# Nine groups of mixer projections a layer as seven products each, with the weight sums on VectorE one group ahead

## The reference, cut to what matters

```python
(sq, sk, sv, dq, dk, dv, iq, ik, iw, hq, hf, hi, hg,
 g_sb, g_dsa, g_hg) = jnp.split(h @ w_in_l, _split_points(), axis=-1)
y_sb = stick_breaking_attention(heads(sq, N_SB), heads(sk, N_SB), heads(sv, N_SB)) @ w_sb_l
y_dsa = dsa_attention(q, k, dv, q_i, k_i, iw) @ w_dsa_l       # keeps the top 64 keys by an index score
o = hgrn2(heads(hq, N_HG), heads(hf, N_HG), heads(hi, N_HG), lb)   # q = silu(hq), a gated recurrence
mixed = sigmoid(g_sb) * y_sb + sigmoid(g_dsa) * y_dsa + sigmoid(g_hg) * y_hg
return mixed @ w_out_l
```

## Time and profile of the kernel before

| | |
|---|---|
| median of 3 runs | 1598.48 us (1598.16 to 1599.77) |
| the profiled execution | 1599.52 us, of it 1597.7 us span |
| PE busy / DVE busy / ACT busy | 1465.1 / 740.9 / 314.8 us |
| mixer steps of layer 0, from the last product of hf (92.31) to the first branch product (249.40) | 157.1 us |
| the same in layer 1 (565.36 to 719.46) | 154.1 us |
| expert weights, from about 1200 us on | DMA at 425 to 427 GB/s |

### The profile page before, as it was taken

One profiled execution on the slowest core, in us unless ns is written; L12 is line 12 of the kernel. 1 busy time (PEld: TensorE's weight loads), 2 busy tenths in 40 slices (PEclk: granted clock), 3 DMA queues, 4 the chain that ended last, 5 costly groups with the idle time before them and its releaser, 6 DMA issues.

```text
span 1597.7 us, 19690 instructions
## 1 busy us (share of the span) xinstructions
PE 1465.1 (92%) x8156; PEld 1006.0 (63%) x8156; DVE 740.9 (46%) x1465; ACT 314.8 (20%) x655; POOL 22.7 (1%) x41
## 2 busy tenths in 40 slices
PE   8999999999999999999999999999999576576578
PEld 5587889999544788898999445755554133133132
DVE  3646576766666646567666656544331000001001
ACT  2234431122001125430222001334410000000000
POOL 0000000000000000000000002200000000000000
PEclk9999999999999999999999999999999788788789
DMA  9547224454443633334444446755799999999997
GB/s 321 187 159 237 95 101 153 161 182 179 158 167 110 218 130 135 106 106 158 158 161 181 186 158 196 232 185 184 288 381 425 427 427 425 428 427 426 427 419 313
DMA packets 114921, 380.17 MB, mean 238 GB/s; under 512 B 10836, under 2 KB 23252, under 8 KB 104144
## 3 DMA queue, kind: packets, MB, share of 16 engines
q1 hardware_dynamic: 111952, 369.53, 60.7%
q0 software_dynamic: 2880, 9.36, 1.9%
HBM read 377.25 MB, written 5.73 MB: 240 GB/s over the span
## 4 chain that ended last, share of the span: by engine, by line
PE 32%; DMA 17%; SPq 1%; DVE 0%; ACT 0%; issue 0%; DVEq 0%
DMA ring<-in_w 17%; PE bank L1495 6%; PE bank L1541 6%; PE bank L1151 4%; PE bank L1692 4%; PE bank L1261 2%; PE bank L1590 2%; PE bank L1718 1%; SPq L928 1%; PE bank L1751 1%; PE bank L1187 1%; PE bank L1213 1%; PE bank L1200 1%; PE bank L1714 1%; PE bank L1648 0%; PE bank L1681 0%
## 5 line engine op out<-in xcount | busy, mean ns | idle before, releaser
L1144 PE MATMUL bank<-hT,ring 128*128 128x256 f32 x832 | 185.4, 381 | 0.0
L1144 PEld LDWEIGHTS bank<-hT,ring 128*128 128x128 f32 x832 | 156.0, 190 | 21.9 <-issue 1.0
L1692 PE MATMUL bank<-ring,region 128*32 128x512 f32 x208 | 115.7, 720 | 50.2 <-DMA region<-in_w 50.2
L1692 PE MATMUL bank<-region 128*32 128x512 f32 x512 | 115.8, 720 | 42.9 <-DMA ring<-in_w 42.9
L1541 PE MATMUL bank<-region 128*128 128x512 f32 x320 | 140.6, 592 | 0.0
L1541 PEld LDWEIGHTS bank<-region 128*128 128x128 f32 x320 | 60.5, 190 | 74.6 <-issue 74.6
L1495 PE MATMUL bank<-region 128*128 128x128 f32 x768 | 100.5, 275 | 0.0
L1495 PEld LDWEIGHTS bank<-region 128*128 128x128 f32 x768 | 93.0, 192 | 0.0
L1692 PEld LDWEIGHTS bank<-region 128*32 128x32 f32 x512 | 28.8, 129 | 87.4 <-issue 87.4
L1692 PEld LDWEIGHTS bank<-ring,region 128*32 128x32 f32 x208 | 25.7, 129 | 85.0 <-issue 85.0
L1751 PE MATMUL bank<-region 128*32 128x512 f32 x192 | 61.9, 748 | 15.7 <-DMA hT<-in_w 13.9
(11 more groups left out here) (486 smaller groups left out, 2413.7 us busy)
## 6 DMA issues: line engine op xcount, KB each, us to landing
region<-in_w SPq DMA_DIRECT2D x43, 2048.0 KB, 38.6
ring<-in_w SPq DMA_DIRECT2D x30, 2048.0 KB, 37.5
ring<-in_w_in SPq DMA_DIRECT2D x26, 2048.0 KB, 8.4
ring<-in_w_up SPq DMA_DIRECT2D x16, 2048.0 KB, 8.3
ring<-in_w_down SPq DMA_DIRECT2D x32, 1024.0 KB, 6.4
own_slot<-in_w SPq DMA_DIRECT2D x7, 2048.0 KB, 43.5
ring<-in_w_out SPq DMA_DIRECT2D x6, 2048.0 KB, 7.8
region<-in_w SPq DMA_DIRECT2D x22, 512.0 KB, 9.0
```

The source lines that it names most:

```text
L1144: t = mm(b[:, 0:T], w[:, k, :], act[:, k, :], start=(k == 0), stop=(k == KD - 1))
L1692: t = mm(b[32 * e:32 * e + 32, :], xg[:, k, 32 * e:32 * e + 32], four[e][c][:, 512 * (k % 2):512 * (k % 2) + 512], start=(k == 0), stop=(k ...
```

## The change

`hq`, `sk` with `sq`, and gate chunks 2 and 3 become nine "early" groups of seven products, numbered 0 to 8; the four groups of gate chunks 4 and 5 become groups 9 to 12. Gate tiles 0 to 7 stay plain. The sums of group n + 1 (`es`, four operations of 512 elements a partition) stand in the list beside the products of group n (`em`), ahead of the corners (`ec`) of group n. The whole-chunk sums `gw` go; `gt` stays, and a third set of row sums, `ge`, is made after `ln`. Groups 0 to 4 use the row sums that hf uses, 5 to 8 use `ge`, 9 to 12 use `gt`.

```diff
-LATE_GATES = 8
+PLAIN_GATES, LATE_GATES = 8, 8
+GROUPS = (("hq", 0), ("hq", 1), ("skq", 0), ("skq", 1), ("skq", 2),
+          (2, 0), (2, 1), (3, 0), (3, 1), (4, 0), (4, 1), (5, 0), (5, 1))
+EARLY, IN_HEADS = 9, 5
+GROUP_SUM = {"m5": 1, "m6": 3, "m7": 3, "m3": 4}
...
+    def em(n, *beside):
+        return [("em", n, m) for m in GATE_ORDER] + list(beside) + [("ec", n), ("ef", n)]
...
-    s += gm("hf", 1, *GATE_ORDER) + [("gc", "hf", 1), ("gf", "hf", 1), ("hq", 0)]
-    s += [("rt", c) for c in range(9)] + [("hj",)] + [("hq", m) for m in range(1, 4)]
+    s += gm("hf", 1, *GATE_ORDER) + [("gc", "hf", 1), ("gf", "hf", 1)]
+    s += [("es", 0)] + [("rt", c) for c in range(9)] + [("hj",)] + em(0, ("es", 1)) + em(1, ("es", 2))
     s.append(("hp",))
     half = N_IDX // 2
-    s += [("ix", 0, j) for j in range(half)] + [("sk", 0)] + [("ix", 0, j) for j in range(half, N_IDX)] + [("tk", 0)]
-    s += [("sk", m) for m in (1, 2)] + [("sq", m) for m in range(3)] + [("t5",)]
+    s += [("ix", 0, j) for j in range(half)] + em(2, ("es", 3))
+    s += [("ix", 0, j) for j in range(half, N_IDX)] + [("es", 4), ("tk", 0)]
+    s += em(3) + em(4) + [("t5",)]
     s += [("ix", 1, j) for j in range(N_IDX)] + [("tk", 1)]
-    s += [("z", c) for c in range(3)] + g(2) + [("ln",)] + g(2)
-    s += [("u", c) for c in range(3)] + g(2) + [("hs",), ("lv", 0), ("lv", 1), ("o", 0), ("o", 1)] + g() + [("o", 2)]
+    s += [("z", c) for c in range(3)] + g(2) + [("ln",), ("ge",)] + g(2)
+    s += [("u", c) for c in range(3)] + g(2) + [("hs",), ("lv", 0), ("lv", 1), ("es", 5), ("o", 0), ("o", 1)] + g() + [("o", 2)]
...
     for j in range(LEVELS):
         n = 3 if j < 4 else 2
-        s.append(("lm", j))
+        if j % 2 == 0:
+            s.append(("lm", j))
         s += att[at:at + n - 1]
         s += [("hx",)] if j == 0 else [("hl", j, 0)] if j < LEVELS - 1 else [("hl", j, 0), ("hl", j, 1)]
         if j + 2 < LEVELS:
             s.append(("lv", j + 2))
         s += att[at + n - 1:at + n]
         at += n
-        s += g(2 if j < 2 else 1)
-
-    s += [("gt",), ("gw", 4), ("ho",)]
+        if j % 2 == 0:
+            s += em(5 + j // 2, *([("lm", j + 1)] if j < LAST else []), ("es", 6 + j // 2))
+        elif j == 1:
+            s += g()
+
+    s += [("es", 10), ("gt",), ("ho",)]
     s += att[18:20] + gm(4, 0, *GATE_ORDER[:4]) + [att[20], ("on",), att[21]] + gm(4, 0, *GATE_ORDER[4:])
-    s += [("gw", 5), ("gc", 4, 0)] + att[22:] + gm(4, 1, *GATE_ORDER) + [("gc", 4, 1), ("gs",), ("gf", 4, 0), ("gf", 4, 1)]
+    s += [("gc", 4, 0), ("es", 11)] + att[22:] + gm(4, 1, *GATE_ORDER) + [("gc", 4, 1), ("es", 12), ("gs",), ("gf", 4, 0), ("gf", 4, 1)]
...
+            def early_product(l, n, m):
...
+                elif m == "m5" and n == IN_HEADS:
+                    pe.wait_ge(row_sums_ready, 3 * l + 2)
+                if m in GROUP_SUM:
+                    pe.wait_ge(group_sums_made, 4 * (len(GROUPS) * l + n) + GROUP_SUM[m])
...
                     elif kind == "z":
...
-                        wait_freed([(l, n, c) for n in ("sq", "sk")])
+                        pe.wait_ge(early_done, EARLY * l + c + 3)
...
+                    elif kind == "ec":
+                        A_(early_corners[:, 6, :], read((l, "ey", s[1]))[:, 0:P], ACT.Copy).then_inc(early_m1, 1)
+                    elif kind == "ef":
...
+                        act.wait_ge(*bk.freed((l, "ey", n)))
+                        if c == "hq":
...
+                            t = A_(hsg_both, early_corners[:, 0:4, :].rearrange("p c t -> p (c t)"), ACT.Sigmoid)
+                        elif c == "skq":
+                            A_(skT[:, t2, :], early_corners[:, 0:2, :].rearrange("p i t -> p (i t)"), ACT.Copy)
+                            t = A_(sqT[:, t2, :], early_corners[:, 2:4, :].rearrange("p i t -> p (i t)"), ACT.Copy, scale=HD ** -0.5)
...
+            def group_weight_sums(l, n):
...
+                elif n >= 2:
+                    dve.wait_ge(*group_done(l, n - 2))
+                (a11, a12), (a21, a22) = group_weights(l, n)
+                s1, s2, s3, s4 = group_sums(l, n)
+                at = 4 * (len(GROUPS) * l + n)
+                V.tensor_tensor(s1, a21, a22, ALU.add).then_inc(group_sums_made, 1)
+                V.tensor_tensor(s3, a11, a21, ALU.subtract).then_inc(group_sums_made, 1)
+                dve.wait_ge(group_sums_made, at + 1)
+                V.tensor_tensor(s2, s1, a11, ALU.subtract).then_inc(group_sums_made, 1)
+                dve.wait_ge(group_sums_made, at + 3)
+                V.tensor_tensor(s4, a12, s2, ALU.subtract).then_inc(group_sums_made, 1)
+
+            def early_corner_sums(l, n):
+
+                if EARLY * l + n >= 1:
+                    dve.wait_ge(early_done, EARLY * l + n)
```

More of the change, by code:

```diff
@@ L845, in gate_sums, with group_weights, group_sums, group_done @@
             own_, a21 = own_quarters, gate_weights(l, c)[1][0]
-            if c in ("hf", 4):
-                return own_[:, 0], own_[:, 1], a21, own_[:, 2]
-            return own_[:, 3], low_quarters[:, 0], a21, low_quarters[:, 1]
+            return own_[:, 0], own_[:, 1], a21, own_[:, 2]
+        def group_weights(l, n):
+            c, t2 = GROUPS[n]
+            if c == "skq":
+                return [[slot(chunk_at[(l, name)])[:, 4 * kh:4 * kh + 4, P * t2:P * t2 + P] for kh in range(2)]
+                        for name in ("sk", "sq")]
+            w = slot(chunk_at[(l, c if c in FM else ("g", c))])
+            return [[w[:, 4 * kh:4 * kh + 4, 256 * fh + P * t2:256 * fh + P * t2 + P] for kh in range(2)] for fh in range(2)]
+        def group_sums(l, n):
+            three = group_sums_at[n % 2 + 2 * (n >= IN_HEADS)]
+            return three[:, 0], three[:, 1], group_weights(l, n)[1][0], three[:, 2]
+        def group_done(l, n):
+            return bk.full((l, "ey", n) if n < EARLY else (l, "gy") + GROUPS[n])
         def row_weights(l, c):
@@ L1342, in _ @@
                 wait_freed([(l, "rsb")])
+                rows = [slice(HD * hh, HD * hh + HD) for hh in range(2)]
                 for s in MIX:
@@ L1357, in _ @@
                         full(t, key)
-                    elif kind in FM:
-                        rows = [slice(HD * hh, HD * hh + HD) for hh in range(2)]
-                        if s[1] == 0:
-                            w = arrived((l, kind))
-                        feature_major(key, w[:, :, P * s[1]:P * s[1] + P], hT)
+                    elif kind == "em":
+                        early_product(l, s[1], s[2])
                     elif kind == "t5":
@@ L2479, in gate_corner_sums @@
                      (l, "gy", c, t2))
+            def group_weight_sums(l, n):
+                for c in {"hq": ("hq",), "skq": ("sk", "sq")}.get(GROUPS[n][0], (("g", GROUPS[n][0]),)):
+                    dve.wait_ge(*arrive[chunk_at[(l, c)]])
+                if n == 1 and l == 0:
+                    dve.wait_ge(kv_stored, 16)
+                elif n >= 2:
+                    dve.wait_ge(*group_done(l, n - 2))
+                (a11, a12), (a21, a22) = group_weights(l, n)
+                s1, s2, s3, s4 = group_sums(l, n)
+                at = 4 * (len(GROUPS) * l + n)
[8 more added lines that the diff above has]
+                    dve.wait_ge(early_done, EARLY * l + n)
+                if 2 * l < EARLY * l + n and n in (1, 2):
+                    dve.wait_ge(hq_made, 2 * l + n)
+                x_, y_ = read((l, "ex", n)), read((l, "ey", n))
+                eight = early_corners.rearrange("p (a b) t -> p a b t", a=2)
+                pairs = early_corners.rearrange("p (a b) t -> p a b t", b=2)
+                m5, m4 = y_[:, P:2 * P], y_[:, 2 * P:3 * P]
+                dve.wait_ge(early_m1, EARLY * l + n + 1)
+                link(V.tensor_tensor(eight[:, :, 0, :], bc(early_corners[:, 6, :].unsqueeze(1), [2, P]),
+                                     x_[:, 0:T].rearrange("p (a t) -> p a t", a=2), ALU.add))
+                free(V.tensor_tensor(eight[:, :, 1, :], bc(early_corners[:, 4, :].unsqueeze(1), [2, P]),
+                                     x_[:, T:2 * T].rearrange("p (a t) -> p a t", a=2), ALU.add), (l, "ex", n))
+                own((l, "ex", n))
+                V.tensor_tensor(pairs[:, 0:2, 1, :], eight[:, :, 1, :], bc(m5.unsqueeze(1), [2, P]), ALU.add)
+                free(V.tensor_tensor(early_corners[:, 2, :], early_corners[:, 5, :], m4, ALU.subtract), (l, "ey", n))
             def down_sums(l, c4):
@@ L2572, in _ @@
                         free(V.tensor_copy(RT[:, s[1], :], read(key)[:, 0:T]), key)
-                    elif kind == "hq":
-                        dve.wait_ge(sig_ready, 6 * l + s[1] + 3)
-                        free(V.tensor_tensor(hqT[:, s[1], :], read(key)[:, 0:T], hsg[s[1] % 2], ALU.mult), key)
+                    elif kind == "es":
+                        group_weight_sums(l, s[1])
+                    elif kind == "ec":
+                        early_corner_sums(l, s[1])
+                    elif kind == "ef" and s[1] < 2:
```

(8 more changed lines are left out.)

89 lines of the change are left out of this document (58 added, 31 removed).

## The result

The changed kernel takes **1645.59 us** (median of 4 runs, 1643.88 to 1646.15), the kernel before 1598.32 beside it: ratio 1.0291, 95% interval 1.0279 to 1.0304. It is 47 us slower. The forecast was 1632 with 1604 to 1652: the direction and the range hold, the value is 14 us short. The profiled execution took 1646.15 us with a span of 1644.4, 46.7 more than before.

What follows compares the result with a forecast made beforehand. TensorE's own work was taken as the bound. New waits of 23.7 and 24.3 us, less old waits and 13.0 saved, gave 29.7; 3.4 for the clock made 33.1 slower: 1632 us, range 1604 to 1652.

Steps and rivals of the forecast that it cites:

- The products: Seven-product groups instead of plain tile pairs: 0.71 us of PE saved per group, 6.5 a layer, 13.0 in all.
- transposes: At the eighth transpose, PE waits 3.3 us a layer for a bank DVE copies behind corners and group 0's sums.
- group 3: At group 3's first bank, which is group 2's: PE waits 2.9 us a layer behind DVE's queue.
- level 4: Before level 4's product: PE waits 4.4 us a layer for DVE's factors, queued behind group 6's corners.
- level 6: Before level 6's product: PE waits 4.4 us a layer for DVE's factors after group 7.
- late row sums: At m5 after group 8: PE waits 2.7 us a layer for row sums behind DVE's corners and sums.
- Place 4: Before the heads: t5 and the second ix wait for banks of groups 3 and 4, 3.9 us layer 0, 4.5 layer 1.
- The clock term: At heads and gate tiles after the longer pause: clock fall costs 1.7 us a layer, 3.4 in all, between 0 and 6.8.
- third rival: Clock falls also at group 3, levels 4 and 6 and late row sums: 13.6 us more, 1645; chance 0.13.
- DVE keeps ahead: At all bank and factor waits: DVE's added work fits its idle time, no waits, 1585.5 us; chance 0.07.
- The levels keep up: Only the first stage waits; waits at levels 4 and 6 and late row sums fall away: 1609 us; chance 0.18.
- the last rival: Sums not ahead of their products: 18 sets of 2.55 us on the path, 46 more, 1678 us; chance 0.02.

Runs made afterwards that it cites:

- af_order2: Whole change, every group, sum and product, in another step order, with hj's copy behind the last transposes, against the kernel before: 1595.67 us, ratio 0.9983.
- af_order: Whole change with only the step order changed, against the kernel before; hj overwrote rows still to be transposed, so not usable: 1604.82 us, ratio 1.0037.
- gt_early: Changed kernel with the late row sums gt moved beside the products of group 8, ahead of its corners: 1634.48 us.
- fill_waits: Changed kernel with throwaway products on TensorE in three waits a layer (level 4, level 6, first late group's m5): 1633.18 us.
- before_w4: Kernel before with VectorE's first product of level 3 made nine more times, so its level factors come late: 1606.78 us, ratio 1.0050.
- heads_only: Changed kernel with groups in the first stage alone (five); gates 0 to 15 plain tiles in the old order: 1613.31 us.
- rt_first: Changed kernel with the sums of group 0 moved behind the transposes and hj on VectorE's queue: 1638.94 us.
- fill_rt: Changed kernel with throwaway products in three waits a layer and group 0's sums moved behind the transposes, together: 1627.63 us.
- ho_order: First stage's groups alone in a reworked step order, hj still overlapping the transposes, against the kernel before: 1606.24 us, ratio 1.0038.
- first_stage2: First stage's groups alone in a mended step order, gates 0 to 15 plain between the levels, against the kernel before: 1599.94 us, ratio 1.0008.
- before_w2: Kernel before with VectorE's first product of level 3 made five more times: 1600.47 us, ratio 1.0014.

## Why the prediction was right, and where it was short

**The products, and DVE's time: right for one group.** A group of seven takes the 6.25 us that the prediction had: the second one of the changed kernel has its first product at 106.87 and its last, 0.89 long, at 112.23. In sum the saving comes out smaller: PE's busy time in the two stretches, less the clock, is 11.9 us below before in the changed kernel and 8.4 in af_order2, not 13.0. Lone small products between the groups' are a part of that (af_order above). DVE +74.9 against 75.

**The places: right in name, a little long in sum.** Forecast against the trace, layer 0: transposes 3.3 and 3.08; group 2 1.4 and 1.48; group 3 2.9 and 2.45; before the heads 3.9 and 0.91; levels 1 and 2 0.7 and 0.39; level 4 4.4 and 4.21; level 6 4.4 and 4.15; late row sums 2.7 and 2.58. Sum 23.7 and 19.25; layer 1 24.3 and 21.0. Seven of eight stand within 0.5 us. Place 4 is the exception, in both layers. VectorE was as late as forecast: group 4's corners end at 141.19, 16.2 us behind the start of group 3, forecast 16.3. But TensorE had work whose banks were free, which the bookkeeping put behind the wait:

```profile
137.67 2.73 PE L1434 MATMUL bank<-region 32*4 32x512 f32 x6
140.33 0.70 PE L1477 MATMUL bank<-region 64*128 64x256 f32 x2
141.24 1.29 PE L1477 MATMUL bank<-region 64*128 64x256 f32 x6 [0.21 <-DVE own_slot L2591]
...
637.47 0.70 PE L1477 MATMUL bank<-region 64*128 64x256 f32 x4 [0.96 <-DVE own_slot L2591]
```

`t5` starts right behind group 4 and lasts 2.7 us; in layer 1 the first four `ix` take its place (635.37, 1.1 us), and group 4 had ended 1.8 later than forecast, behind a fall at group 3. The slow clock at the heads of layer 0 (0.57) is not the reason: it is full there in layer 1 and in gt_early's layer 0, and the waits are 1.7 and 1.0 us, far below the forecast too. The old waits were 1.1 and 1.7, not 3.0 and 2.3. Net, 42.7 forecast and 37.5 measured: 5.2 too many. The queue that makes level 4 wait is as the prediction lists it, in the timeline of DVE:

```profile
206.42 0.28 DVE L2591 TENSOR_TENSOR own_slot<-own_slot,bank 128x128 f32<-128x128 f32 x1
...
207.04 0.76 DVE L2828 COPY_PREDICATED region<-region,bank 128x256 f32<-128x256 uint32 x2
207.70 0.68 DVE L2787 TENSOR_TENSOR region<-region 128x512 f32<-128x512 f32 x1
...
209.10 0.61 DVE L2306 TENSOR_SCALAR region<-region,small 128x256 f32<-128x256 f32 x2
...
210.30 0.68 DVE L2811 TENSOR_TENSOR region<-region 128x512 f32<-128x512 f32 x1
```

Corners of group 6, masked copy, exponents, normalising, factors, end to end, while TensorE has nothing left of its level.

**The clock term: the step that failed.** The forecast had 2 x 1.7 = 3.4 us more for it, at the heads alone, with an upper end of 6.8. Measured are 23.9, less the 1.7 that before had: 22.2. The unit was right, 1.7 us; their number was not: thirteen more than before (fourteen against one) instead of two more, and only in layer 0 are any at the heads, where both layers were forecast to have one. The measured terms are 37.5 - 11.9 + 22.2 = 47.7 in the two stretches, of which 1.0 comes back elsewhere, against 33.1: the clock was 18.8 short and the products about 1, and the waits, 5.2 too long, hid part of that. That the value still fell within the range is in part this luck.

This is the third rival's mechanism, named at 1645 with a chance of 0.13. Its number came out by two errors that cancel: ten units more than before where there are thirteen, 5.2 us short, on waits that were 5.2 us too long. What spoke against it in the prediction, "the waits are half as long as a fall and return", names no row. The rows that could have been read were the dip of the earlier trace rows around small products without a long wait: the clock had fallen there with no long wait at all. fill_waits and before_w4 show the mechanism by itself.

The Trainium skill, TensorE: Matmul & The Clock Gate, in the section on HAM oscillation, tells of a kernel whose products wait for data again and again and that pays the fall each time instead of once. This trace agrees: fourteen units in two layers, paid again at five places of each. Beyond the page, the traces here show that the same wait can bring the fall in one layer and not in the other.

**The other rivals.** "DVE keeps ahead" (1585.5) was the least likely for this list, but af_order2 at 1595.7 is its case: other places for the same steps make most of it true. "The levels keep up" (1609) is nearly heads_only (1613.3), whose clock losses make the difference. No set of sums was late at a m5, so the last rival falls.

## What to carry to other kernels

Before work goes onto an engine with idle time, walk its queue in order and ask who waits for the step behind; a busy share of 50% said nothing here, and the list of eight waits did. Then price each wait twice, as idle time and as a clock that may fall behind it: 1.7 us or twice that, as dear as the wait itself where that is 1.5 to 4 us. And if a change with a true saving comes out slower, try the order before the idea: the same instructions took 1645.6 us in one order and 1595.7 in another.

## What was not expected of the hardware

- The clock fell behind the waits of 4.15 to 4.22 us every time (both layers of the changed kernel, rt_first and gt_early), behind 2.97 in both layers of af_order, and behind 3.10 in one layer of two (before_w4). Behind the wait of 2.45 at group 3 it fell in nine of the twelve layers of the six kernels that have it (changed, fill_waits, heads_only, rt_first, gt_early, fill_rt). In the changed kernel it is one of two. The timeline of PE of the changed kernel, layer 1, to be read against its line at 125.00 above (2.02 us):

```profile
621.07 3.45 PE L1379 MATMUL bank<-hT,ring 128*128 128x128 f32 x16 [2.45 <-DVE own_slot L2591]
```

- It also fell behind waits of 1.4 to 1.6 us where small products lay around them: the transposes (1.52, in seven of eight layers; here 3.46 for sixteen passes), the index products in ho_order (1.39, then 3.60) and in layer 0 of af_order2 and of first_stage2 (1.60 and 1.61; 3.43 and 3.04), but not in layer 1 of either or of af_order (1.61 each). Behind the wait of 1.48 at group 2 it never did, and not behind 1.26 in before_w2. So the length of a wait alone does not decide; what else does, these runs leave open.
- The time lost came in steps of 1.7 us in every kernel of the table. Behind the waits of 4.2 it was one step or two (level 4 of the changed kernel: one in layer 0, two in layer 1).
